# Thirty-two experts taken one at a time, in quarters of columns, instead of two at a time in halves

## The chip, the cores and the metric

The kernel runs on one core of one Trainium2 chip. The metric is the device time of one execution in microseconds; the time of a kernel is the median of its runs.

## What is computed

The reference is two layers over 512 tokens of width 1024; the change is in the first layer's mixture of experts. Each token takes its 4 best of 32 experts. An expert's gate and up weights are 1024 x 2048, its down weights 1024 x 1024, all in float32:

```
logits = xt @ w_router + b_router
top_val, top_idx = top_k(logits, 4); gates = softmax(top_val)
gate, up = split(xb @ w_gu[e] + b_gu[e])        # xb: the rows of xt that chose expert e
gate = min(gate, 7); up = clip(up, -7, 7)
hb = (up + 1) * gate * sigmoid(1.702 * gate)
yb = hb @ w_down[e] + b_down[e]                  # summed per token, weighted by its gates
```

All weights of all experts are read once from HBM: 32 x 12 MiB = 402.7 MB.

## The kernel before

An expert gets a list of at most CAP = 96 tokens, in NR = 3 rounds of ROUND = 32 rows (an expert with more would go through a second loop in `moe_exit`, behind a flag). `project_and_route` (L3433) makes the normed rows `xn`, stores them to the DRAM tensor `hidden` (512 x 1024), computes the logits with `w_router` and the table `members` of each token's rank in each expert.

`experts` (L1128) then works through 16 groups of two experts. The PE array is used as four column groups of 32 columns each: group q multiplies 32 rows (the stationary operand, 128x32) with 512 columns of weights (the moving operand) and writes 32 partitions of a PSUM bank. Before the change, the four groups are two experts times two halves of 1024 columns. For a group of experts:

- `list_rows` (L1228) multiplies one-hots of the ranks (`mark_group`, L1122, on DVE) with token numbers, and `next_index` (L1384) on DVE turns the result into row indices. POOL fetches the rows of x with one indirect DMA for each expert (L1196), 96 rows of 4 KB.
- `turn_x` (L1208) transposes x on PE against the identity, 16 transposes a group in four sets, and ACT copies the result out of PSUM (`copy_x`, L1340).
- `gate_up` (L1242): for each of 8 row blocks k, 6 banks (gate and up, three rounds) times 4 column groups, 192 matmuls; then 24 bias matmuls, four behind each bank's last block.
- `swiglu` (L1398) on DVE, with the sigmoid on ACT (L1352), in 12 DVE steps of 512 columns.
- `turn_h` (L1219) transposes h on PE, 12 transposes in three sets, and ACT copies them (`copy_h`, L1347).
- `down` (L1272): 96 matmuls of 512 columns, into the three gate banks; `copy_y` (L1414) copies them out on DVE, and ACT's queue stores them to `expert_table` (`y_out`, L1357) in four DMAs of 192 KB, pieces of 2 KB.

PE's order is written out by hand: `step` (L1295) runs `gate_up` of group e with the list of group e+1 and the transposes of h of group e-1 hooked in, then `down` of group e-1 with the transposes of x of group e+1 hooked in.

Weights come in units of 1 MiB through SP's queue (L1176) into 12 slots: six of the ring that the whole kernel shares (`weight_ring`) and six more (`more_weights`). A load waits until PE has released its slot (`ring.used`); PE releases two units at a time, since it works on two experts' units at once:

```
            def landed(n, e=None):
                for i in (n, n + 1):
                    sem, count = landing(i)
```

The units of the ring after the experts' are those of the next layer (`plan`, L3752).

## Time and profile before

| | us |
|---|---|
| median of 3 runs (lowest, highest) | 2746.55 (2745.76, 2748.36) |
| the profiled execution | 2733.44 |
| its span, first to last instruction | 2731.6 |
| PE busy in it | 2548.1 (93%) |
| DVE busy | 933.4 (34%) |
| ACT busy | 701.4 (26%) |
| POOL busy | 136.8 (5%) |

The profile is of one execution. The span runs from its first to its last instruction. Busy time of PE counts from the start of a matmul to its modelled end, and matmuls overlap, so 93% is not 93% of what the array can do; what counts is how far apart matmuls start. PEld is PE's load of the stationary operand. An f32 matmul appears as two matmul records and two loads. SPq and ACTq are the instructions with which SP and ACT start DMAs. The mean granted clock of PE over the span is 0.972 of 2.4 GHz.

### The profile page before, as it was taken

Reading aid. Unit: us, or ns where it says so; the run is one execution under the profiler, and the core shown is the slowest. Engines: PE = TensorE matmul, PEld = TensorE weight load, DVE = VectorE, ACT = ScalarE, POOL = GpSimd, SP = SyncE. Lnnn points to the kernel's source line nnn. Section 1 sums busy time; section 2 is a strip of 40 time slices with the busy share of each in tenths; the row PEclk is TensorE's granted clock in tenths of the full one; section 3 lists DMA queues with packets and bytes.
Section 4 is the critical chain, followed back from the end, with each engine's and each line's share of the span. In section 5 each row is a group of like instructions: output and inputs, shape, how many; then the busy total and the mean of one; then the engine's idle time right before and its main releaser. Section 6 shows DMA issues by size and latency. Waiting matters only on the chain. (4 is left out here: it accounts for less than half of the span.)

```text
span 2731.6 us, 49644 instructions
## 1 busy us (share of the span) xinstructions
PE 2548.1 (93%) x21426; PEld 1501.2 (55%) x21426; DVE 933.4 (34%) x1449; ACT 701.4 (26%) x1275; POOL 136.8 (5%) x110
## 2 busy tenths in 40 slices
PE   8989987999999999999999789879888799899998
PEld 6658754333333333333333258656677677788887
DVE  5575253111111111111111153547645434422233
ACT  4353331000000000000000142347555223422222
POOL 0003000000000000000000010001122000000000
PEclk9989998999999999999999989999999899999999
DMA  5343223999999999999999743421100323122220
GB/s 209 116 167 128 104 83 124 401 408 406 396 393 391 393 389 394 391 390 391 389 395 394 269 162 110 169 96 54 50 4 4 136 89 139 47 93 93 103 98 31
DMA packets 115976, 587.00 MB, mean 215 GB/s; under 512 B 12640, under 2 KB 14432, under 8 KB 71200
## 3 DMA queue, kind: packets, MB, share of 16 engines
q1 hardware_dynamic: 98944, 539.07, 51.1%
q10 hardware_dynamic: 11008, 24.98, 2.5%
q0 software_dynamic: 5888, 20.97, 2.2%
q8 instruction: 106, 1.74, 0.3%
q14 instruction: 30, 0.25, 0.0%
HBM read 564.00 MB, written 20.97 MB: 214 GB/s over the span
## 5 line engine op out<-in xcount | busy, mean ns | idle before, releaser
L1261 PE MATMUL psum<-weight_ring,expert_xT 128*32 128x512 f32 x3120 | 347.8, 597 | 1.5 <-ACT expert_xT L1344 1.5
L1261 PE MATMUL psum<-more_weights,expert_xT 128*32 128x512 f32 x3024 | 347.4, 593 | 0.0
L368 DVE TENSOR_TENSOR w_low<-weight_ring,w_high 128x2048 fp32r<-128x2048 f32 (+1 forms) x92 | 213.4, 2321 | 322.6 <-ACT w_high L363 322.2
L363 ACT CAST w_high<-weight_ring 128x2048 fp32r<-128x2048 f32 (+1 forms) x88 | 166.6, 1893 | 290.5 <-PE psum L402 144.2
L1261 PEld LDWEIGHTS psum<-weight_ring,expert_xT 128*32 128x32 f32 x3120 | 99.0, 110 | 221.2 <-issue 220.8
L1402 DVE TENSOR_SCALAR gate<-psum 128x512 f32<-128x512 f32 x48 | 33.2, 692 | 540.8 <-PE psum L1268 540.8
L1261 PEld LDWEIGHTS psum<-more_weights,expert_xT 128*32 128x32 f32 x3024 | 95.5, 110 | 196.7 <-issue 190.0
L1288 PE MATMUL psum<-more_weights,expert_hT 128*32 128x512 f32 x1584 | 178.7, 594 | 0.0
L1350 ACT COPY expert_hT<-psum 128x512 f32<-128x512 f32 x48 | 28.0, 586 | 537.1 <-PE psum L1225 511.6
L1288 PE MATMUL psum<-weight_ring,expert_hT 128*32 128x512 f32 x1488 | 165.8, 594 | 0.0
L402 PE MATMUL psum<-mix_hT_high,w_high 128*128 128x512 f32 x384 | 156.0, 406 | 6.5 <-PEq L1981 3.5
L406 PE MATMUL psum<-mix_hT_high,w_low 128*128 128x512 f32 x384 | 150.9, 393 | 0.0
L405 PE MATMUL psum<-mix_hT_low,w_high 128*128 128x512 f32 x384 | 150.8, 393 | 0.0
L402 PE MATMUL psum<-ffn_x_high,w_high 128*128 128x512 f32 x352 | 138.3, 393 | 3.8 <-PEq L3258 3.8
L405 PE MATMUL psum<-ffn_x_low,w_high 128*128 128x512 f32 x352 | 137.9, 392 | 0.0
L406 PE MATMUL psum<-ffn_x_high,w_low 128*128 128x512 f32 x352 | 137.9, 392 | 0.0
L1419 DVE COPY expert_y<-psum 128x512 f32<-128x512 f32 x48 | 33.2, 691 | 280.5 <-PE psum L1288 279.6
L1288 PEld LDWEIGHTS psum<-more_weights,expert_hT 128*32 128x32 f32 x1584 | 49.1, 110 | 101.5 <-issue 97.0
L1288 PEld LDWEIGHTS psum<-weight_ring,expert_hT 128*32 128x32 f32 x1488 | 45.5, 110 | 97.3 <-issue 94.0
L1196 POOL DMA_INDIRECT expert_x<-hidden,index x32 | 38.0, 1186 | 1100.9 <-DVE index L1388 912.4
L1344 ACT COPY expert_xT<-psum 128x384 f32<-128x384 f32 x64 | 30.4, 478 | 231.0 <-PE psum L1216 231.0
L1355 ACT ACTIVATE sigmoid<-gate 128x512 f32<-128x512 f32 x48 | 30.3, 630 | 229.3 <-DVE gate L1402 229.3
(540 smaller groups left out, 4040.9 us busy)
## 6 DMA issues: line engine op xcount, KB each, us to landing
weight_ring<-in_w_gu SPq DMA_DIRECT2D x130, 1024.0 KB, 8.3
more_weights<-in_w_gu SPq DMA_DIRECT2D x126, 1024.0 KB, 7.0
more_weights<-in_w_down SPq DMA_DIRECT2D x66, 1024.0 KB, 10.1
weight_ring<-in_w_down SPq DMA_DIRECT2D x62, 1024.0 KB, 9.2
weight_ring<-in_w_in SPq DMA_DIRECT2D x35, 1024.0 KB, 5.1
weight_ring<-in_w_ada SPq DMA_DIRECT2D x24, 1024.0 KB, 4.8
weight_ring<-in_w_ffn_in SPq DMA_DIRECT2D x22, 1024.0 KB, 4.8
expert_table<-expert_y ACTq DMA_DIRECT2D x64, 192.0 KB
```

What stands on the lines that cost most here:

```text
L363: self.m.nc.scalar.copy(high, w).then_inc(self.rounded.sem, 1)
L368: self.m.nc.vector.tensor_tensor(low, w, high.bitcast(F32), ALU.subtract).then_inc(self.ready.sem, 1)
L402: ins = m.nc.tensor.matmul(out, w[0][:, k, c], x[0][:, k, 0:n], start=(k == 0), stop=False)
L405: m.nc.tensor.matmul(out, w[0][:, k, c], x[1][:, k, 0:n], start=False, stop=False)
L406: ins = m.nc.tensor.matmul(out, w[1][:, k, c], x[0][:, k, 0:n], start=False, stop=(k == ktiles - 1))
L1196: nc.gpsimd.indirect_dma_start(x[i][:, :], None, hidden, bass.IndirectOffsetOnAxis(ap=ix[0:CAP, i:i + 1], axis=0)).then_inc(gathered[i].se ...
L1261: ins = T.matmul(ps[NR * up + j][quarter(q), :], xT[:, k, i, quarter(j)], w[i][:, up * D + c * 512:up * D + (c + 1) * 512], start=(k == 0) ...
L1288: ins = T.matmul(ps[j][quarter(z), :], hT[:, q % 2 * 2 + r, j, quarter(2 * i + q // 2)], w[i][:, r * D + c * 512:r * D + (c + 1) * 512], s ...
L1344: nc.scalar.copy(xT[:, 4 * c:4 * c + 4, i, :], ps[6 + c][:, 0:4 * CAP].rearrange("p (k s) -> p k s", k=4)).then_inc(x_copied.sem, 1)
L1355: nc.scalar.activation(s[:, j, :], g[:, j, :], ACT.Sigmoid, scale=1.702).then_inc(sig_done.sem, 1)
L1402: V.tensor_scalar(g[:, j, :], ps[j][:, :], 7.0, None, ALU.min).then_inc(gate_ready.sem, 1)
L1419: V.tensor_copy(y[:, j, :], ps[j][:, :]).then_inc(y_copied.sem, 1)
```

## The change

Experts are taken one at a time. The four column groups are now four quarters of one expert's columns. The columns of a quarter are not contiguous: quarter q holds the columns 128k + 32q to 128k + 32q + 31 of every block k (`by_quarters`), so that the 32x32 block transpose of DVE puts h into the order in which `down` needs it. For x the same order is made by storing `hidden` permuted (and the router's rows with it), viewing it as 2048 quarter rows of 1 KB, and fetching quarter q of a row into partitions 32q to 32q + 31: three indirect DMAs of 128 quarter rows for each expert. DVE then turns x and h, six transposes of 128x256 an expert, and PE's transposes and ACT's copies of them go. `gate_up` uses three banks instead of six (gate in columns 0 to 255, up in 256 to 511), `down` has three banks of its own, and swiglu and y's copy run over all three banks in one instruction of 768 columns. The list needs 12 small matmuls an expert instead of 8 a group. PE releases one unit at a time. PE's order is `gate_up` of expert e, with the list of expert e+1 two units in, then `down` of expert e-1. `moe_exit` gets a reordering copy in the loop behind its flag. The core of the diff:

```diff
 def gate_up_units(dram, e):
-    return [dram["w_gu"][e(i), k * P:(k + 1) * P, :] for k in range(GUN) for i in range(EG)]
+    return [dram["w_gu"][e, k * P:(k + 1) * P, :] for k in range(GUN)]
...
+def by_quarters(z):
+    return z.rearrange("p (k q c) -> p k q c", q=NQ, c=ROUND)
+
+def mark_ranks(nc, oc, iota, members, e):
+    for j in range(NR):
+        last = nc.vector.tensor_tensor(oc[:, :, j, :].rearrange("p t (q i) -> p t q i", q=NQ),
...
+def list_rows(nc, bank, oc, tok):
+    for j in range(NR):
+        for t in range(NT):
+            last = nc.tensor.matmul(bank[:, 2 * j:2 * j + 2], oc[:, t, j, :], tok[:, 2 * t:2 * t + 2], start=(t == 0), stop=(t == NT - 1))
...
             def gather():
-                for i in range(EG):
-                    nc.gpsimd.indirect_dma_start(x[i][:, :], None, hidden, bass.IndirectOffsetOnAxis(ap=ix[0:CAP, i:i + 1], axis=0)
+                for j in range(NR):
+                    nc.gpsimd.indirect_dma_start(x[:, j, :], None, hidden, bass.IndirectOffsetOnAxis(ap=ix[:, j:j + 1], axis=0)
...
+                        if k == 0:
+                            pe.wait_ge(x_ready.sem, e * NR + x_ready.at(j + 1))
+                            if j == 0 and loop is not None:
+                                pe.wait_ge(gate_ready.sem, loop + gate_ready.at(0))
+                                pe.wait_ge(gu_freed.sem, loop + gu_freed.at(0))
+                        for q in range(NQ):
+                            ins = T.matmul(ps[j][part(q), :], xT[:, j, k, :], w[:, :, q, :], start=(k == 0), stop=False)
+                            if j == 0 and q == 0:
+                                release(ins, n0 + k)
+                    if k == GUN - 1:
+                        for j in range(NR):
+                            for q in range(NQ):
+                                ins = T.matmul(ps[j][part(q), :], sel[:, :], by_quarters(bias[:, :])[:, :, q, :], start=False, stop=True)
...
+                            for q in range(NQ):
+                                ins = T.matmul(y_banks[part(q), j, :], hT[:, j, 2 * k + r, :], w[:, r * D + q * QD:r * D + (q + 1) * QD],
+                                               start=(k == 0 and r == 0), stop=(k == DNN - 1 and r == 1))
...
+            gate_up(0, 0, half_way=lambda: make_list(0))
+            gate_up(GUN, 1, 1, lambda: make_list(1))
+            down(GUN + GUN, 0)
+            with pe.Fori(2, LAST) as e:
+                gate_up(GUN, e, e, lambda: make_list(e))
+                down(GUN + GUN, e - 1, e)
+            gate_up(GUN, LAST, LAST)
+            down(GUN + GUN, LAST - 1, LAST)
+            down(N - DNN, LAST)
...
+            def turn_x(e):
                 for j in range(NR):
+                    dve.wait_ge(gathered[j].sem, e * 16 + gathered[j].at(16))
+                    V.transpose(xT[:, j, :, :].rearrange("p k s -> p (k s)"), x[:, j, :]).then_inc(x_ready.sem, 1)
...
+            def leave_banks(e):
+                dve.wait_ge(gu_done.sem, e + gu_done.at(1))
+                V.tensor_scalar(g[:, :, :], gate_up_banks[:, :, 0:QD], 7.0, None, ALU.min).then_inc(gate_ready.sem, 1)
+                V.tensor_scalar(u[:, :, :], gate_up_banks[:, :, QD:2 * QD], 7.0, -7.0, ALU.min, ALU.max).then_inc(gu_freed.sem, 1)
...
             with dve.Fori(1, LAST) as e:
+                next_index(e)
+                marks(bass.ds(e + 2, 1))
+                leave_banks(e)
+                turn_x(e + 1)
+                mark(bass.ds(e + 1, 1))
                 swiglu(e)
+                copy_y(e - 1)
+                turn_h(e)
...
-            sp.dma_start(wr[:, :, :].rearrange("p k e -> p (k e)"), m.dram["w_router"]).then_inc(loaded.sem, 16)
+            for k in range(KD):
+                q = slice(ROUND * (k % 4), ROUND * (k % 4) + ROUND)
+                sp.dma_start(wr[q, k // 4:KD:2, :], m.dram["w_router"].rearrange("(q c) (k e) -> k c q e", q=NQ, k=KD)[k]).then_inc(loaded.sem, 16)
...
-                    V.scalar_tensor_tensor(xn[t % 2][:, half(h)], m.X[:, t, half(h)], stat[:, t, 4:5], row[:, half(h)],
-                                           ALU.mult, ALU.mult).then_inc(scaled.sem, 1)
+                    for q in (2 * h, 2 * h + 1):
+                        last = V.scalar_tensor_tensor(xn[t % 2][:, q * QD:(q + 1) * QD].rearrange("p (k c) -> p k c", k=KD),
+                                                      by_quarters(m.X[:, t, :])[:, :, q, :], stat[:, t, 4:5], by_quarters(row[:, :])[:, :, q, :],
+                                                      ALU.mult, ALU.mult)
+                    last.then_inc(scaled.sem, 1)
```

## Rows read from the trace of the kernel before

**Rows 1.** The page, the span in 40 slices of 68.3 us each.

```profile
GB/s 209 116 167 128 104 83 124 401 408 406 396 393 391 393 389 394 391 390 391 389 395 394 269 162 110 169 96 54 50 4 4 136 89 139 47 93 93 103 98 31
```

**Rows 2.** Waits of PE and of SP's queue, 500 to 1580 us: total, times, longest.

```profile
PE psum L1225 <- ACT expert_hT L1350: 2.8, 1, 2.8
...
SPq L1176 <- PE psum L1261: 511.4, 120, 8.6
```

**Rows 3.** Windows: length, busy time (instructions) of each engine, PEclk, DMA share, GB/s.

```profile
480.00:700.00 220.00, 218.86 (x2056) 70.79 (x2052) 39.24 (x67) 19.34 (x35) 6.89 (x6) 1.00 1.02 407
700.00:1500.00 800.00, 800.00 (x7436) 254.78 (x7432) 124.72 (x212) 63.88 (x115) 25.28 (x22) 1.00 1.00 392
```

**Rows 4.** Timeline of SP's queue, 455 to 720 us: start, length, instruction.

```profile
461.15 0.33 SPq L1176 DMA_DIRECT2D weight_ring<-in_w_gu  x1
...
554.43 13.07 SPq L1176 DMA_DIRECT2D more_weights<-in_w_gu  x6
...
622.79 13.07 SPq L1176 DMA_DIRECT2D more_weights<-in_w_gu  x6
```

**Rows 5.** Timeline of PE and its loads in one group, and at the stage's end.

```profile
1281.94 0.66 PE L1225 MATMUL psum<-ident,up 128*128 128x128 f32 x4
...
1287.82 0.66 PE L1225 MATMUL psum<-ident,up 128*128 128x128 f32 x4
...
1300.66 0.40 PE L1268 MATMUL psum<-bias,sel_gu 96*32 96x512 bf16 x4
...
1301.74 0.40 PE L1268 MATMUL psum<-bias,sel_gu 96*32 96x512 bf16 x4
...
1313.66 0.55 PE L1216 MATMUL psum<-ident,expert_x 96*128 96x96 f32 x4
...
1316.85 0.55 PE L1216 MATMUL psum<-ident,expert_x 96*128 96x96 f32 x4
...
1332.57 0.13 PEld L1261 LDWEIGHTS psum<-weight_ring,expert_xT 128*32 128x32 f32 x4 [0.30 <-issue]
...
1333.99 0.16 PEld L1261 LDWEIGHTS psum<-more_weights,expert_xT 128*32 128x32 f32 x8
...
1334.44 0.13 PEld L1261 LDWEIGHTS psum<-more_weights,expert_xT 128*32 128x32 f32 x4 [0.30 <-issue]
...
1334.87 0.13 PEld L1261 LDWEIGHTS psum<-more_weights,expert_xT 128*32 128x32 f32 x4 [0.30 <-issue]
...
1539.99 15.63 PE L1288 MATMUL psum<-more_weights,expert_hT 128*32 128x512 f32 x144
```

**Rows 6.** Timeline of PE in other stages.

```profile
100.13 0.39 PE L3210 MATMUL psum<-w_high,hT_high 128*128 128x512 f32 x1
...
101.49 0.39 PE L3210 MATMUL psum<-w_high,hT_high 128*128 128x512 f32 x1
...
125.47 1.07 PE L1824 MATMUL psum<-weight_ring,silu_c 128*32 128x256 f32 x16
...
2200.49 0.39 PE L402 MATMUL psum<-mix_hT_high,w_high 128*128 128x512 f32 x1
...
2201.85 0.39 PE L402 MATMUL psum<-mix_hT_high,w_high 128*128 128x512 f32 x1
```

**Rows 7.** A window of the recurrence, in the columns of rows 3.

```profile
2000.00:2010.00 10.00, 9.27 (x314) 8.11 (x312) 5.39 (x13) 6.10 (x19) 5.64 (x6) 1.00 0.01 3
```

**Rows 8.** DMA, 460 to 700 us: packets, MB, share; issues, us to landing.

```profile
q0 software_dynamic: 896, 3.15, 4.1%
q10 hardware_dynamic: 896, 1.57, 1.8%
...
expert_x<-hidden,index POOLq DMA_INDIRECT x8, 10.6
```

**Rows 9.** Groups by form, 530 to 1560 us: busy, mean ns | idle before.

```profile
L1402 DVE TENSOR_SCALAR gate<-psum 128x512 f32<-128x512 f32 x45 | 31.1, 692 | 513.2 <-PE psum L1268 513.2
...
L1196 POOL DMA_INDIRECT expert_x<-hidden,index x26 | 29.9, 1149 | 858.8 <-DVE index L1388 854.8 <-issue 4.0
```

More of the change, by code:

```diff
@@ L62 @@
 DNN = 4
-GROUPS = E // EG
 EXTRA = 6
@@ L1235, in landed @@
-            def landed(n, e=None):
-                for i in (n, n + 1):
-                    sem, count = landing(i)
-                    pe.wait_ge(sem, count if e is None else (e - 1) * (16 * LOOP // SLOTS) + count)
-                return slot(n), slot(n + 1)
-            def gate_up(n0, group, e=None, hook=lambda k: None):
+            def landed(n, e=None):
+                sem, count = landing(n)
+                pe.wait_ge(sem, count if e is None else (e - 1) * (16 * LOOP // SLOTS) + count)
+                return slot(n)
@@ L1244, in gate_up, with release @@
+            def release(ins, n):
+                if n > 0 or U0 > 0:
+                    ins.then_inc(ring.used, 1)
+            def gate_up(n0, e, loop=None, half_way=lambda: None):
                 for k in range(GUN):
[L1245 to L1248 removed]
+                    w = by_quarters(landed(n0 + k, loop))
+                    if k == 2:
+                        half_way()
@@ L1352, in sigmoid @@
-            def sigmoid(group):
-                for j in range(NR):
-                    act.wait_ge(gate_ready.sem, group * NR + gate_ready.at(j + 1))
-                    nc.scalar.activation(s[:, j, :], g[:, j, :], ACT.Sigmoid, scale=1.702).then_inc(sig_done.sem, 1)
-            def y_out(group, e):
-                act.wait_ge(y_copied.sem, group * NR + y_copied.at(NR))
-                for z in range(4):
-                    i, c = z // 2, z % 2
-                    dst = table[e(i), :, c * 512:c * 512 + 512]
-                    dst = dst.rearrange("(j p) n -> p j n", p=ROUND) if len(dst.shape) == 2 else dst.rearrange("a (j p) n -> p (a j) n", p=ROUND)
-                    act.dma_start(dst, y[quarter(z), :, :]).then_inc(y_stored.sem, 16)
@@ L1365, in _, with sigmoid, y_out @@
-            copy_x(0)
+            def sigmoid(e):
+                act.wait_ge(gate_ready.sem, e + gate_ready.at(1))
+                nc.scalar.activation(s[:, :, :], g[:, :, :], ACT.Sigmoid, scale=1.702).then_inc(sig_done.sem, 1)
+            def y_out(n, e):
+                act.wait_ge(y_copied.sem, n + y_copied.at(1))
+                for q in range(NQ):
+                    dst = table[e, :, q * QD:(q + 1) * QD]
+                    dst = dst.rearrange("a (j p) n -> p (a j) n", p=ROUND) if len(dst.shape) == 3 else dst.rearrange("(j p) n -> p j n", p=ROUND)
+                    act.dma_start(dst, y[part(q), :, :]).then_inc(y_stored.sem, 16)
@@ L1414, in copy_y @@
-            def copy_y(group, e=None):
-                for j in range(NR):
-                    dve.wait_ge(down_done.sem, group * NR + down_done.at(j + 1))
-                    if j == 0 and e is not None:
-                        dve.wait_ge(y_stored.sem, group * 64 + y_stored.at(0))
-                    V.tensor_copy(y[:, j, :], ps[j][:, :]).then_inc(y_copied.sem, 1)
-            dve.sem_inc(y_copied.sem, NR)
-            dve.sem_inc(y_stored.sem, 1)
-            mark(slice(0, EG))
-            mark_ranks(slice(EG, 2 * EG))
@@ L3528, in _ @@
             pe.wait_ge(onehot.sem, onehot.at(1))
-            for i in range(EG):
-                for t in range(NT):
-                    last = T.matmul(ps[5][0:CAP, 2 * i:2 * i + 2], oc[:, t, i, :], tok[:, 2 * t:2 * t + 2], start=(t == 0), stop=(t == NT - 1))
-            last.then_inc(listed.sem, 1)
+            list_rows(nc, ps[5], oc, tok).then_inc(listed.sem, 1)
         @block.scalar
@@ L3593, in _ @@
             V.memset(members[:, :, E:E + 2], 0.0)
+            for q in range(NQ):
+                V.memset(quarter[ROUND * q:ROUND * q + ROUND, :], float(q))
             def copy_turned(t):
```

333 lines of the change are left out of this document (121 added, 212 removed).

## The prediction

> **What bounds the kernel now.** I read the page first for where the time lies. In the slices of GB/s [rows 1] one stage stands out: for some 1100 of 2731.6 us the core moves about 390 GB/s. That is the expert stage, 16 groups of two experts, the only stage whose loops change. There I read the waits [rows 2]. TensorE (PE) waits once, 2.8 us for a copy of h at the very end; the SP queue waits 511.4 us for PE's gate and up matmuls alone, that is, for slots to come free. So PE sets the pace and weights wait for it. The windows [rows 3] say how near the loads are to being the bound: PE is busy throughout, and the 16 DMA engines show 1.00 to 1.02. From 480 to 700 us, while the late start of the loads was caught up, they moved 407 GB/s; later, when SP had to wait, 392. I take 407 as what they can do with this mix and 392 as what PE asks for. Third, the period: SP's issues repeat 554.43 to 622.79 [rows 4], 68.36 us a group.
>
> The PE timeline [rows 5] splits that period. An f32 matmul is two records; four records, one for each column group, start each 0.43 us (1334.44 to 1334.87). A group of experts has 288 matmuls, 576 records, 144 rounds of 0.4295 = 61.8 us. The rest is what PE does in between:
> - h transposes: 1281.94 to 1287.82 is 5.88 us for 48 records (12 rounds, 5.15) and one set of transposes: 0.73, three times, 2.2 us.
> - x transposes: 1313.66 to 1316.85 is 3.19 for 24 records (6 rounds, 2.58): 0.61, four times, 2.4 us.
> - bias: 1300.66 to 1301.74 is 1.08 for 2 rounds (0.86) and 4 bias matmuls: 0.22, six times, 1.3 us.
> - the list of rows: 1332.57 to 1334.44 is 1.87 for 3 rounds (1.29): 0.58.
>
> Sum 68.3, against 68.36. It closes, so PE's stage is counted out.
>
> **The change on PE.** Per pair of experts:
> - Gate and up: 96 matmuls an expert of 512 columns, 192 a pair, as before: 384 records, 96 rounds, 41.2 us, if the moving operand costs the same. It is now 16 runs of 32 columns. The nearest rows are the wide tiles, whose moving operand is two runs of 256: six records in 1.36 us (100.13 to 101.49), exactly as the unbroken L402, six in 1.36 (2200.49 to 2201.85) [rows 6]. One break costs nothing. From the other side, 0.227 less the 0.215 of a pass here is 0.012 us, the most one break could have cost, were the unbroken row slow for another reason. I take zero, and keep 12 ns a break.
> - Down: 192 matmuls of 256 columns in place of 96 of 512, 96 rounds of half the columns. From below a round is half of 0.43, 0.215; from above it is a quarter of L1824's 1.07 us, in which 16 records of just this shape run, the last one's way out of the array included [rows 6]: 0.27. I take 0.215, since that tail comes once a group and not once a round: 20.6 us, as before; at 0.27 it would be 25.7.
> - Bias: 24 matmuls, 1.3 us. Lists: 12 matmuls where 8 cost 0.58, so 0.87, twice a pair, 1.7 us.
> - The x and h transposes, 4.6 us, leave PE.
>
> Sum 64.9: 3.5 us less, over 16 pairs 56 us. That is what PE alone would give.
>
> Down's records now go out twice as often, one load and one matmul record each 54 ns. A stretch of small matmuls shows 314 records and 312 loads in 10 us [rows 7], 32 ns, so I cost the issue at nothing. The Trainium skill ("TensorE: Matmul & The Clock Gate", on decode and dispatch) gives about 62 ns per MATMUL where the sequencer decodes in software; by that, down would be 384 x 62 ns = 23.8 us, PE 68.1, and the gain near nothing. By that rule the trace does not go here: it shows half of that.
>
> **The change on the loads.** A pair moves 24 weight units (25.17 MB), 0.79 MB of x and 0.79 MB of y: 26.7 MB, at 407 GB/s 65.7 us. So the next thing to be late is the weights, just behind PE's 64.9. Pieces shrink to 1 KB: x from 192 pieces of 4 KB to 768, y from 384 of 2 KB to 768. The queue rows [rows 8] cover 240 us times 16 engines: ACT's stores take 1.8%, 69 us, for 768 data packets of 2 KB, 90 ns each or 44 ns per KB; the fetches 4.1%, 157 us, for 768 packets of 4 KB, 205 ns or 50 ns per KB (the other 128 packets of each are completion counts; I give them no time). A 1 KB piece costs at least its bytes, 41 to 45 ns, and at most what a 2 KB one does, 90. At the upper end: 384 more stores (35 us) and 768 x 90 - 192 x 205 = 30 us of fetches, 65 over 16 engines, 4.0 us a pair. At the lower end nothing. Time has been near the bytes in both rows, so I take 0.2 us: 65.9 us a pair, with 65.7 and 69.7 as ends.
>
> From the first issue of the stage at 461.15 [rows 4], when five units are in place, 379 units (397.4 MB), 31 experts' x (12.2) and 30 experts' y (11.8) must move before the last unit is in: 421.4 MB / 407 GB/s = 1035 us, plus 3 for the pieces and 2 for the first landing, so 1501; PE uses the last unit in 2.6: 1504. PE's last matmul now ends at 1539.99 + 15.63 = 1555.6 [rows 5]. So 51.6 us by the loads, 56 less the start-up below by PE.
>
> **What moves to other engines.** VectorE (DVE) does the turning: six block transposes of 256 columns an expert. DVE's 512-column PSUM read is 0.69 us [rows 9], so some 0.35 each, and 1.0 for each of the five 768-column steps; with marks and index near 9.5 us of 32.5. Its order puts the x turning between the bank copies and the swiglu, and y's copy ahead of the h turning: h for expert e is ready about 2 us into gate_up(e+1) and wanted 20 us later. ACT loses its 7 copies a group. Costed at nothing under PE's 32 us an expert.
> The x chain is the one to watch. The list of expert e+1 runs two units into gate_up(e), 5.2 us; index by about 7; POOL's three fetches at 1.15 us [rows 9] and the gaps between, the last issued near 10; landing 10.6 us after issue [rows 8], so 21. DVE turns x near 24, PE wants it at 32. Cover: 8 us. SP issues 12 loads an expert one slot at a time, unhindered.
> Once only: gate_up(1) follows gate_up(0) with no down between, so two bank copies and one turning are bare: 2.0 + 0.35 and the handshakes, 2.7 us lost. Before the last down, y's copy and a turning (1.4 us) stand where transposes and their copies stood: nothing. Ahead of the first gate_up, longer marks and a longer list (0.3 on PE, some 1 on DVE) stand against four sets of x transposes and their copies that go (2.4): nothing. The router table comes as eight small loads: seven more issues on SP, ahead of weights needed 70 us later, and perhaps 2 us for DVE under a PE tile; the four xn steps for two: nothing.
>
> **Sum.** PE 56 - 2.7 = 53; loads 52. The two paces meet so closely that each will now and then wait for the other; I take 50 us. Against the profiled execution, 2733.44 us (its span 2731.6), that is 2683.4. It ran 13.1 us under the median of the three runs; the forecast for the median is 2746.55 - 50 = 2696.5 us. Less than 0.2%, 5.5 us, I call no change.
>
> **Rivals.**
> - **Broken reads slow the gate and up matmuls: slower.** Place: the moving operand in 1536 rounds (16 pairs x 96), each with 30 breaks (15 in each pass). At the bound of 12 ns a break: 0.36 us a round, +553 us, 2746.6 - 50 + 553 = 3250. It decides from 50/1536 = 33 ns a round, 1.1 ns a break. For: no row has runs so short. Against: the wide tiles. The Trainium skill ("Advanced Engine Details and Errata", Memory Cachelines) says that any non-contiguous access pattern significantly slows matmuls, though under PSUM; under SBUF it speaks of 16-byte lines and asks for two hits on each. Here PSUM stays contiguous and a run is 128 bytes, so its SBUF rule would leave the time alone. 0.10.
> - **Small pieces fill the queues.** At 69.7 us a pair the loads pass today's 68.36, +21 us less the start's credit: about 2760. Break-even is 68.2, some 2.5 us a pair, 40 engine-us over 960 more pieces, 42 ns each. For: 1.02 of share is already used. Against: 44 and 50 ns per KB in pieces of 2 and 4 KB. Over break-even 0.07; around it, no change, 0.06; part of the gain eaten (2715 to 2741), 0.12.
> - **The three fetches land late.** If a landing grew to 10.6 us for each fetch one after the other, x is in at 7 + 32 = 39, turned at 40, 8 us after PE wants it: 32 x 8 = 256 us, about 2950. For: three where two were, 128 pieces each. Against: 10.6 us is what they took in the stretch in which the weights' own queue ran at its full 407 GB/s [rows 3, 8]. 0.04.
> - **Issue binds down: slower.** At the upper bound of 0.27 a round, 25.7 us, PE's pair is 70.0 against 68.36: 16 x 1.6 + 2.7, about 2775. It decides from 0.25 a round, 62 ns a record. For: L1824 shows no more than four rounds in a row. Against: rows 7. (The software decode that the Trainium skill describes, cited above, would end just there.) 0.01.
> - **PE and loads as summed.** 2682 to 2715: 0.60.
>
> **Numbers.** Faster 0.60 + 0.12 = 0.72; same 0.06; slower 0.10 + 0.07 + 0.04 + 0.01 = 0.22. The range runs from all of PE's gain and a little at the start, 2680, to the packets' upper end, 2765; outside are most of the broken-read, issue and fetch cases, under 0.2.
>
> **What would show it.** In the changed profile: no L1216 or L1225 transposes; rounds of 0.43 us in gate and up and 0.215 in down; SP's period near 32.8 us an expert; GB/s near 407 through the whole stage and first PE waits for weights, short ones. Wrong would be: rounds over 0.46 us in gate and up (broken reads); GB/s under 400 with SP no longer waiting for PE (pieces); PE or DVE waiting on expert_x (fetches).

## The result and the profile after

The changed kernel takes 2669.08 us (median of four runs, 2661.5 to 2671.59) against 2746.16 before: a ratio of 0.9718, 95% interval 0.9693 to 0.9742, so 77 us less, give or take 7. The forecast was 2696.5 with a range of 2680 to 2765. The sign was right and the result lies below the range. The profiled executions, 2733.44 and 2661.5 us, differ by 71.9; the traces account for that, and the further 5.1 us between the medians are scatter of single executions.

The page's GB/s slices of the changed kernel answer to [rows 1], and its windows (in the columns of [rows 3]) to [rows 3]:

```profile
GB/s 204 111 178 139 111 42 102 414 416 417 416 417 416 417 416 416 416 416 416 416 416 416 299 114 80 190 72 43 45 4 47 111 91 127 56 102 95 95 95 32
```

```profile
480.00:700.00 220.00, 217.61 (x2720) 87.31 (x2716) 62.89 (x121) 6.67 (x8) 21.23 (x21) 1.00 1.02 416
700.00:1400.00 700.00, 700.00 (x8896) 284.95 (x8891) 193.03 (x373) 17.78 (x22) 66.71 (x66) 1.00 1.02 416
```

The stage moves 416 GB/s in both windows; 407, which the prediction took for the loads' limit, is passed at once. The waits of TensorE and, in a second fence, of SP's queue answer to [rows 2] (waited for: us in all, times, longest):

```profile
PE psum L1254 <- DVE expert_xT L1337: 9.2, 2, 6.8
PE psum L1497 <- PEq L1188: 6.4, 1, 6.4
...
PE psum L1538 <- DMA exit_b_down<-in_b_down: 2.7, 1, 2.7
```

```profile
SPq L1198 <- PE psum L1254: 524.4, 252, 7.5
SPq L1198 <- PE psum L1274: 246.0, 120, 2.2
```

TensorE waits for no weight in the whole stage. Its 9.2 us are the first turned x of the stage (6.8) and the bare hand-over at the second expert (2.4). SP still waits for TensorE. The timeline of TensorE at the stage's first matmul, through one expert in its middle, and at its end answers to [rows 5]:

```profile
456.79 7.54 PE L1254 MATMUL psum<-weight_ring,expert_xT 128*32 128x512 f32 x48 [6.79 <-DVE expert_xT L1337]
...
901.10 5.33 PE L1254 MATMUL psum<-more_weights,expert_xT 128*32 128x512 f32 x48
906.37 0.45 PE L1145 MATMUL psum<-tok,rank_onehot 128*128 128x2 bf16 x12
906.75 5.36 PE L1254 MATMUL psum<-more_weights,expert_xT 128*32 128x512 f32 x48
911.92 10.48 PE L1254 MATMUL psum<-weight_ring,expert_xT 128*32 128x512 f32 x96
922.22 0.83 PE L1260 MATMUL psum<-bias,sel_gu 96*32 96x512 bf16 x12
922.88 5.36 PE L1274 MATMUL psum<-weight_ring,expert_hT 128*32 128x256 f32 x96
928.06 5.36 PE L1274 MATMUL psum<-more_weights,expert_hT 128*32 128x256 f32 x96
933.24 5.33 PE L1254 MATMUL psum<-more_weights,expert_xT 128*32 128x512 f32 x48
...
1480.64 10.57 PE L1274 MATMUL psum<-more_weights,expert_hT 128*32 128x256 f32 x192 [1.48 <-DVE expert_hT L1361]
1497.63 1.92 PE L1497 MATMUL psum<-ident,dense_gates 128*32 128x128 f32 x16 [6.42 <-PEq L1188]
1502.28 3.79 PE L1538 MATMUL psum<-exit_b_down,exit_gates_T 32*128 32x512 f32 x8 [2.73 <-DMA exit_b_down<-in_b_down]
```

The steps can be read off. Gate and up: 96 records in 10.30 us (911.92 to 922.22), 24 rounds of 0.429, as before the change, though the operand is now in runs of 32 columns. Down: 96 records in 5.18 us (922.88 to 928.06), 24 rounds of 0.216, half of 0.43. An expert takes 901.10 to 933.24, 32.14 us: 64.3 a pair where 68.36 stood [rows 4]. From the first expert matmul to the end of the last, the stage is 456.79 to 1491.21, 1034.4 us, against 459.23 to 1555.62, 1096.4, before. I call this the length of the stage. It is read from one execution of each kernel, but it repeats far better than the whole time: where nothing in the stage should change, it comes out the same to 0.2 us (1096.4 and 1096.3, 1024.0 and 1023.8 below).

So 62.0 of the 71.9 us come from the stage. The start differs by 2.4, which is scatter (over all runs below it lies between 451.9 and 462.5). The remaining 7.5 come behind the stage, all but 0.1 of them in two waits right behind it, where the kernel before had (timeline of TensorE, the answers to the last two rows above):

```profile
1564.81 1.92 PE L1548 MATMUL psum<-ident,dense_gates 128*32 128x128 f32 x16 [9.19 <-PEq L1166]
1574.10 3.79 PE L1589 MATMUL psum<-exit_b_down,exit_gates_T 32*128 32x512 f32 x8 [7.37 <-issue]
```

The last stores are waited for 2.8 us less, and the matmuls of the exit bias 4.6 us less. What these two are worth is taken up at the end.

The transfers from 460 to 700 us answer to [rows 8]:

```profile
q0 software_dynamic: 1152, 3.15, 3.5%
q10 hardware_dynamic: 2688, 2.36, 2.9%
...
more_weights<-in_w_gu SPq DMA_DIRECT2D x34, 1024.0 KB, 17.7
...
expert_x<-hidden,index POOLq DMA_INDIRECT x24, 5.8
```

The same 3.15 MB of x took 4.1% of the engines before and take 3.5% now, in fewer packets than its 3072 pieces of 1 KB: 24 x 16 = 384 of the 1152 are counts, as before, which leaves 768 packets of 4 KB. The pieces are packed together. A fetch, now a third of the bytes, lands 5.8 us after its issue, not 10.6. Weights land 17.7 us after theirs, some seven units of 1 MB queued at 2.5 us each. The loads are close behind TensorE.

### The profile page after: what moved, and what is told of

Same layout as the page of the kernel before. It is cut to its first block and busy times, and to the rows that moved or that the text cites. A ratio compares the mean times of both kernels' runs of the same rounds, so it can differ in the third digit from the quotient of the medians.

```text
span 2659.7 us, 55822 instructions
## 1 busy us (share of the span) xinstructions
PE 2483.8 (93%) x24306; PEld 1570.6 (59%) x24306; DVE 1042.5 (39%) x1703; ACT 640.1 (24%) x1147; POOL 196.5 (7%) x174
## 5 line engine op out<-in xcount | busy, mean ns | idle before, releaser
L1301 ACT ACTIVATE sigmoid<-gate 128x768 f32<-128x768 f32 x32 | 27.0, 843 | 991.3 <-DVE gate L1343 991.3
L1343 DVE TENSOR_SCALAR gate<-psum 128x768 f32<-128x768 f32 x32 | 30.7, 958 | 451.8 <-PE psum L1260 451.8
L1274 PE MATMUL psum<-more_weights,expert_hT 128*32 128x256 f32 x3168 | 176.8, 379 | 1.5 <-DVE expert_hT L1361 1.5
L1216 POOL DMA_INDIRECT expert_x<-hidden,index x96 | 98.3, 1024 | 1060.0 <-DVE index L1326 855.6
L1274 PE MATMUL psum<-weight_ring,expert_hT 128*32 128x256 f32 x2976 | 166.3, 379 | 0.0
L1274 PEld LDWEIGHTS psum<-more_weights,expert_hT 128*32 128x32 f32 x3168 | 103.9, 110 | 68.7 <-issue 1.9
L1274 PEld LDWEIGHTS psum<-weight_ring,expert_hT 128*32 128x32 f32 x2976 | 96.3, 110 | 64.7
L1356 DVE COPY expert_y<-psum 128x768 f32<-128x768 f32 x32 | 30.6, 957 | 185.1 <-PE psum L1274 185.1
L402 PEld LDWEIGHTS psum<-mix_hT_high,w_high 128*128 128x128 f32 x384 | 73.0, 190 | 27.4 <-issue 12.7
L405 PEld LDWEIGHTS psum<-mix_hT_low,w_high 128*128 128x128 f32 x384 | 72.9, 190 | 17.4 <-issue 2.6
## 6 DMA issues: line engine op xcount, KB each, us to landing
weight_ring<-in_w_gu SPq DMA_DIRECT2D x130, 1024.0 KB, 17.4
more_weights<-in_w_gu SPq DMA_DIRECT2D x126, 1024.0 KB, 17.7
more_weights<-in_w_down SPq DMA_DIRECT2D x66, 1024.0 KB, 18.9
weight_ring<-in_w_down SPq DMA_DIRECT2D x62, 1024.0 KB, 18.2
weight_ring<-in_w_in SPq DMA_DIRECT2D x35, 1024.0 KB, 5.8
weight_ring<-in_w_ada SPq DMA_DIRECT2D x24, 1024.0 KB, 4.9
weight_ring<-in_w_ffn_in SPq DMA_DIRECT2D x22, 1024.0 KB, 4.8
```

The lines of the kernel that those rows point to most:

```text
L402: ins = m.nc.tensor.matmul(out, w[0][:, k, c], x[0][:, k, 0:n], start=(k == 0), stop=False)
L405: m.nc.tensor.matmul(out, w[0][:, k, c], x[1][:, k, 0:n], start=False, stop=False)
L1216: nc.gpsimd.indirect_dma_start(x[:, j, :], None, hidden, bass.IndirectOffsetOnAxis(ap=ix[:, j:j + 1], axis=0)).then_inc(gathered[j].sem, 16)
L1274: ins = T.matmul(y_banks[part(q), j, :], hT[:, j, 2 * k + r, :], w[:, r * D + q * QD:r * D + (q + 1) * QD], start=(k == 0 and r == 0), sto ...
L1301: nc.scalar.activation(s[:, :, :], g[:, :, :], ACT.Sigmoid, scale=1.702).then_inc(sig_done.sem, 1)
L1343: V.tensor_scalar(g[:, :, :], gate_up_banks[:, :, 0:QD], 7.0, None, ALU.min).then_inc(gate_ready.sem, 1)
```

## The experiments

The theory after this reading: TensorE sets the pace of the changed kernel, and 407 GB/s was no property of the loads but held the cost of the old fetch of x. Rivals: the loads still bind, at 416; or 407 came from something else in the old order. All runs follow, with the stage's length from each trace, from the start of the first expert matmul to the end of the last. The ratio is to the kernel before, run beside it.

| Run | Median us | Ratio, 95% interval | Stage us |
|---|---|---|---|
| before | 2746.16 | 1 | 1096.4 |
| after | 2669.08 | 0.9718 (0.9693 to 0.9742) | 1034.4 |
| a_no_bias | 2664.24 | 0.9704 (0.9674 to 0.9734) | 1024.1 |
| a_short | 2661.97 | 0.9714 (0.9680 to 0.9747) | 1024.0 |
| a_rows4k | 2682.44 | 0.9779 (0.9738 to 0.9819) | 1044.0 |
| a_short_rows4k | 2682.33 | 0.9773 (0.9744 to 0.9802) | 1043.1 |
| b_no_turns | 2688.28 | 0.9813 (0.9781 to 0.9846) | 1049.3 |
| b_no_turns_quarters | 2669.81 | 0.9737 (0.9716 to 0.9758) | 1032.2 |
| b_quarters | 2741.16 | 0.9995 (0.9977 to 1.0012) | 1096.3 |
| a_short_fixed1k | 2668.05 | 0.9719 (0.9674 to 0.9765) | 1023.8 |
| a_short_rows3k | 2670.24 | 0.9749 (0.9728 to 0.9770) | 1020.7 |
| a_short_split4k | 2701.38 | 0.9834 (0.9785 to 0.9883) | 1055.2 |
| a_short_part96 | 2683.40 | 0.9800 (0.9756 to 0.9845) | 1042.8 |
| a_short_down8k | 2658.83 | 0.9682 (0.9634 to 0.9729) | 1015.5 |
| a_down8k | 2716.17 | 0.9892 (0.9846 to 0.9937) | 1074.1 |
| a_list4 | 2668.75 | 0.9744 (0.9724 to 0.9763) | 1032.0 |
| a_pairs | 2667.95 | 0.9734 (0.9714 to 0.9754) | 1034.4 |
| a_pairs_list4 | 2668.24 | 0.9740 (0.9717 to 0.9763) | 1031.8 |

### How far are the loads behind TensorE?

**a_no_bias**: the bias matmuls of the experts are left out.

```diff
-  ... xT[:, j, k, :], w[:, :, q, :], start=(k == 0), stop=False)
+  ... xT[:, j, k, :], w[:, :, q, :], start=(k == 0), stop=(k == GUN - 1))
-  for q in range(NQ):
-      ins = T.matmul(ps[j][part(q), :], sel[:, :], by_quarters(bias[:, :])[:, :, q, :], ...)
```

> The changed kernel without the twelve bias matmuls of each expert (the expert gate and up biases are left out of the result). They take some 0.6 us of TensorE's 32.14 us an expert. Theory TensorE alone sets the pace and the loads have room above 416 GB/s: 31.5 us an expert, 32 x 0.6 = 20 us less, about 2649 us, some 424 GB/s, and TensorE waits for no weights. Rival, the loads are at their limit at 416 GB/s (both meet): within 3 us of 2669, 32.1 us an expert, and TensorE waits for weights. In between (a limit near 420): about 2659.

Of the 21 us taken from TensorE (0.66 an expert) the stage gives back 10.3. The timeline shows why. Two lists that follow each other early in the stage, and two late:

```profile
521.36 0.45 PE L1145 MATMUL psum<-tok,rank_onehot 128*128 128x2 bf16 x12
...
552.84 0.45 PE L1145 MATMUL psum<-tok,rank_onehot 128*128 128x2 bf16 x12
...
1315.43 0.45 PE L1145 MATMUL psum<-tok,rank_onehot 128*128 128x2 bf16 x12
...
1347.53 0.45 PE L1145 MATMUL psum<-tok,rank_onehot 128*128 128x2 bf16 x12
```

Early an expert takes 31.48 us, TensorE's own pace without the bias, while the weights already on the chip are used up. Late it takes 32.10 (32.07 on average over the last 15), the pace of the loads, against 32.14 in the changed kernel. The two paces all but meet, and what was gained was gained early: of the twelve slots seven are queued (17.7 us at 2.5), so some four units lie ready besides the one in use, 4 x 2.5 = 10 us (an estimate), and these are spent once. The time between the two theories comes from that stock.

**a_short**: the last of eight steps of gate and up cut to one matmul of twelve.

```diff
-  for q in range(NQ):
+  for q in range(NQ if k < GUN - 1 else j == 0):
       ins = T.matmul(ps[j][part(q), :], xT[:, j, k, :], ...)
```

> The changed kernel with the last of the eight steps of each gate and up product cut to one matmul of twelve (that part of the sum is left out), every weight still loaded. TensorE then needs about 2.2 us less an expert, 59.9 us a pair of experts, so that the loads should bind and show their limit: 26.74 MB a pair. If the limit is 416 GB/s: 64.3 us a pair, no gain, 2669 us. If it is 422: 63.4 a pair, 14 us less, 2655. If there is none below 446 GB/s: 59.9 a pair, 70 us less, 2599. My theory is a limit near 422. In the case of a limit TensorE waits for weights in every expert; otherwise in none.

The window from 700 to 1400 us (columns of [rows 3]), and TensorE's waits for weights:

```profile
700.00:1400.00 700.00, 673.77 (x8420) 299.17 (x8416) 192.94 (x370) 18.58 (x22) 66.69 (x66) 1.00 1.02 417
```

```profile
PE psum L1274 <- DMA weight_ring<-in_w_down: 24.7, 26, 1.0
PE psum L1254 <- DMA weight_ring<-in_w_gu: 5.2, 24, 0.3
```

TensorE now waits for weights in 26 and 24 places and the stage is as long as without the bias, 1024.0. That is the loads' limit with this mix: 417 GB/s, not the 422 I held likeliest. It is a quarter of a per cent above what the changed kernel moves.

### Does the shape of the fetch move the limit?

**a_rows4k**: from the third expert on, one fetch of 96 whole rows at fixed places into a spare tile.

```diff
-  for j in range(NR):
-      indirect_dma_start(x[:, j, :], None, hidden, ...(ap=ix[:, j:j + 1], axis=0))
+  indirect_dma_start(spare[:, :], None, whole, ...(ap=at[0:CAP, 0:1], axis=0))
```

> The changed kernel, with the three quarter fetches of an expert replaced from the third expert on by one fetch of 96 whole 4 KB rows at fixed places into a spare tile (the same 393 KB; x keeps its old contents, so the experts compute on old rows). Theory: the 407 GB/s of the kernel before held the cost of this fetch shape. Then the fetches dent the loads again, 26.74 MB / 407 = 65.7 us a pair, 16 x 1.4 = 23 us more, about 2692, and TensorE waits for weights after fetches. Rival, the shape of the fetch costs the loads nothing and 407 came from elsewhere: 2669 within 3 us, 416 GB/s, no wait for weights.

**a_short_rows4k**: both edits together.

> Both edits of the two runs before together: the last step of each gate and up product cut to one matmul of twelve, and one fetch of 96 rows of 4 KB in place of three of 128 quarter rows. With TensorE at about 59.9 us a pair the loads bind, so the cost of the fetch shape stands free of TensorE. Theory fetch shape: 407 GB/s, 65.7 us a pair, some 37 us above the run with the short step and quarter fetches if that one is at 422 GB/s. Rival, the shape costs nothing: within 3 us of that run.

The same window of the one and of the other:

```profile
700.00:1400.00 700.00, 694.49 (x8816) 281.44 (x8812) 193.21 (x373) 17.83 (x22) 24.18 (x22) 1.00 1.02 408
```

```profile
700.00:1400.00 700.00, 663.84 (x8294) 294.95 (x8290) 188.30 (x363) 17.73 (x21) 23.13 (x21) 1.00 1.02 409
```

Same bytes, same order, same weights: 408 and 409 GB/s in place of 416 and 417. With the short step the stage grows from 1024.0 to 1043.1, 19 us (expected 37 from a limit of 422 that was not there). a_rows4k loses 9.6 us in the stage where 23 were expected, since TensorE again lives on its stock at first. The theory holds: the old fetch costs the loads 2% more than the new one. The queues' shares from 700 to 1400 us tell where it falls: the weights' queue takes 95.3% of the 16 engines' time for 274.36 MB in a_short and 94.8% for 269.62 MB in a_short_rows4k, which is 38.9 and 39.4 us of one engine for each MB; the fetches' queue takes 40 and 47. With 12.58 MB of weights and 0.39 MB of x an expert, more than half of the cost lies in the weights' own packets.

The same from the other side. **b_no_turns** takes the transposes alone out of the kernel before.

```diff
-  for k in range(4):
-      last = T.transpose(ps[6 + c][:, k * CAP:(k + 1) * CAP], x[i][...], ...)
-  last.then_inc(x_turned.sem, 1)
+  return x_turned      # counted up by the next matmul; h likewise
```

> The kernel before with TensorE's transposes of x and h left out of its loop (the copies to xT and hT then take what lies in the banks, so the experts compute on old data); waits, copies, fetches of 4 KB rows and loads stay. TensorE alone would then need about 63.7 us a pair of experts in place of 68.4. Theory: with the fetch of before the loads go to 409 GB/s, 26.74 MB / 409 = 65.4 us a pair, some 15 x 3.0 = 45 us less than the kernel before. Rival, the loads go to 417 here too: 64.1 us a pair, 64 us less. Rival, TensorE alone: 63.7, 70 us less.

**b_no_turns_quarters** adds quarter rows:

```diff
-  indirect_dma_start(x[i][:, :], None, hidden, ...(ap=ix[0:CAP, i:i + 1], axis=0))
+  for j in range(NR):
+      indirect_dma_start(spare[:, i, j, :], None, whole, ...(ap=at[:, 0:1], axis=0))
```

> The same, and from the third pair on x is fetched as six fetches of 128 quarter rows (1 KB, fixed places, into a spare tile) in place of two of 96 rows of 4 KB. Theory, the fetch shape sets the limit of the loads: 417 GB/s, 64.1 us a pair, about 64 us less than the kernel before and some 19 us less than the run with whole rows. Rival, the shape matters only beside the rest of the change: equal to that run within 4 us.

**b_quarters** has the new fetches and keeps the transposes.

> The kernel before with its transposes, and only the fetches replaced by six of 128 quarter rows at fixed places into a spare tile from the third pair on (the experts compute on old rows). TensorE sets the pace of before at 68.4 us a pair, 391 GB/s, below either limit. Theory: equal to the kernel before within 4 us. Rival, the loads already bound before: up to 20 us less.

Lists of b_no_turns that follow each other, early and late, and those of b_no_turns_quarters:

```profile
516.60 0.52 PE L1236 MATMUL psum<-tok,rank_onehot 128*96 128x2 bf16 x8
...
580.31 0.52 PE L1236 MATMUL psum<-tok,rank_onehot 128*96 128x2 bf16 x8
...
1296.31 0.52 PE L1236 MATMUL psum<-tok,rank_onehot 128*96 128x2 bf16 x8
...
1361.59 0.52 PE L1236 MATMUL psum<-tok,rank_onehot 128*96 128x2 bf16 x8
```

```profile
515.54 0.52 PE L1251 MATMUL psum<-tok,rank_onehot 128*96 128x2 bf16 x8
...
579.25 0.52 PE L1251 MATMUL psum<-tok,rank_onehot 128*96 128x2 bf16 x8
...
1280.66 0.52 PE L1251 MATMUL psum<-tok,rank_onehot 128*96 128x2 bf16 x8
...
1344.92 0.52 PE L1251 MATMUL psum<-tok,rank_onehot 128*96 128x2 bf16 x8
```

Without transposes TensorE needs 63.71 us a pair at first, as the prediction's counts give (68.3 less 4.6). But with the old fetch the loads hold it to 65.28 later and only 47 us of the stage are gained (1049.3). With quarter rows it keeps 63.71 until near the end, when the stock is used up and a pair takes 64.26, and 64 are gained (1032.2), as much as the whole change gives (62.0), with the old stores and the old order of loads. Quarter rows alone give nothing (1096.3), since TensorE needs 68.36. Neither part does the work alone: the transposes take TensorE off the path, and the new fetch lets the loads follow.

### What in the fetch costs the loads?

All with the short step, so that the loads bind. **a_short_fixed1k** is the control: three fetches of 128 quarter rows at fixed places.

> A control for the runs with fixed rows: the short last step, and three fetches of 128 quarter rows of 1 KB per expert as in the changed kernel, but at fixed places and into a spare tile. Theory, the shape of the fetch counts and not which rows it takes: equal to the run with the short step alone within 4 us, 417 GB/s. Rival, fixed rows spread over the table are what costs: near the run with one fetch of 96 whole rows, 20 us more.

**a_short_split4k**: three fetches of 32 rows of 4 KB.

> The short last step, and the 96 whole rows of 4 KB fetched by three fetches of 32 rows each instead of one of 96 (fixed places, spare tile). If it is the 4 KB row into one partition that costs the loads: 408 GB/s, as with one fetch of 96, 20 us more than with quarter rows. If it is one large fetch that takes all its packets at once: near 417 GB/s, within 5 us of the run with quarter rows. My chance for the row is six in ten.

**a_short_rows3k**: one fetch of 128 rows of 3 KB.

> The short last step (one matmul of twelve in the last step of gate and up), and one fetch of 128 rows of 3 KB at fixed places into a spare tile, the same 393 KB on all 128 partitions. If the length of the row taken by one partition is what costs the loads: near 408 GB/s, some 15 to 20 us above the run with the short step and quarter rows. If it is that a fetch of 96 or 32 rows leaves partitions out: 417 GB/s, within 5 us of that run.

**a_short_part96**: four fetches of 96 partitions in 1 KB pieces.

```diff
+  for j in range(NQ):
+      indirect_dma_start(spare[:, j, :], None, whole, ...(ap=at[0:CAP, 0:1], axis=0))
```

> The short last step, and the same 393 KB fetched by four fetches of 96 partitions, each partition taking 1 KB quarter rows at fixed places (spare tile), in place of three fetches of 128. If leaving partitions out is what costs the loads: the stage from the first expert matmul to the last takes some 1043 us as with 96 rows of 4 KB (with 128 partitions it was 1024 with quarter rows and 1021 with rows of 3 KB), 20 us more in all, near 2682. If it is the 4 KB row: 1024 us, near 2665.

The window from 700 to 1400 us of each, in this order:

```profile
700.00:1400.00 700.00, 674.91 (x8392) 297.80 (x8388) 194.12 (x374) 18.58 (x22) 66.74 (x66) 1.00 1.02 417
```

```profile
700.00:1400.00 700.00, 654.81 (x8178) 290.60 (x8174) 186.03 (x357) 17.75 (x21) 58.94 (x63) 1.00 1.02 403
```

```profile
700.00:1400.00 700.00, 674.26 (x8432) 303.09 (x8428) 194.86 (x374) 18.58 (x22) 25.15 (x22) 1.00 1.02 418
```

```profile
700.00:1400.00 700.00, 663.33 (x8270) 293.58 (x8266) 190.16 (x366) 17.72 (x21) 83.36 (x87) 1.00 1.02 409
```

The control is as long as a_short (417 GB/s, 1023.8 against 1024.0): fixed places and the spare tile cost nothing. The length of the row, for which I gave six chances in ten, is not it: 3 KB rows on 128 partitions cost no more than 1 KB rows there (418 GB/s, the stage 1020.7), and 1 KB pieces on 96 partitions cost as much as 4 KB rows on 96 (409, 1042.8). Which rows are read is not it either: part96 takes the first 96 of the 128 quarter rows that the control takes. With 32 rows in a fetch it is worse (403, 1055.2, where I expected 408 or 417). Its three fetches go to three different sets of 32 partitions, so that an expert's bytes lie on the same 96 partitions as with one fetch of 96: what counts is how many partitions one fetch takes. Against fetches of all 128, the same 393 KB an expert cost 19 us more over the stage in fetches of 96 partitions and 31 in fetches of 32. That it is the partitions of a fetch is shown for 128 and 96, since on either the length of the row and the number of fetches could be changed at next to no cost; for 32 it rests on one run. How they cost the loads is not shown.

The Trainium skill ("SBUF — State Buffer", on the DMA port swizzle) says that a transfer's rate depends on how many of sixteen ports its partitions reach, and that the first 64 partitions lie on eight of them. By that, a fetch of 32 rows loads eight ports alone, and one of 96 loads these twice as much as the others. The order of the four runs agrees; no run shows the ports.

### Longer pieces for down

**a_short_down8k** and **a_down8k** give each partition two neighbouring rows of w_down, 8 KB, and let TensorE read every second column of gate and up to match.

```diff
-  ... z.rearrange("a (c p) n -> p (a c) n", p=P)
+  ... z.rearrange("a (p c) n -> p (a c n)", p=P)
-  return z.rearrange("p (k q c) -> p k q c", q=NQ, c=ROUND)
+  return z.rearrange("p (k q c r) -> p q k r c", q=NQ, c=ROUND, r=2)
```

> The changed kernel with its short last step (one matmul of twelve, as before), and the w_down units laid so that a partition takes two neighbouring rows, 8 KB in one piece, in place of two of 4 KB; gate and up columns are read in pairs to match (every second column, 8 bytes apart). Theory: the loads bind this kernel and pieces of 8 KB go faster, as the gate and up units do: about 422 GB/s, 63.4 us a pair, 12 us below the run with the short step alone. Rival, the limit does not depend on the piece: equal within 4 us. Rival, TensorE reads columns 8 bytes apart at half its rate: then it binds and the run is hundreds of us longer.

> The changed kernel with all its matmuls, and only the w_down units in pieces of 8 KB with gate and up columns read in pairs; nothing is left out. Theory: TensorE takes 64.2 us a pair by itself, so that a higher limit of the loads gives back next to nothing: within 4 us of the changed kernel, with transfers that land sooner after their issue than its 17 to 19 us. Rival, the loads alone set the pace of the changed kernel: 12 us less. Rival, reads 8 bytes apart slow TensorE: hundreds of us more.

The window of a_short_down8k, then one group of matmuls from 700 to 1400 us in a_down8k and in the changed kernel (busy, mean ns | idle):

```profile
700.00:1400.00 700.00, 699.55 (x8561) 313.09 (x8550) 196.85 (x378) 18.57 (x22) 66.70 (x66) 1.00 1.02 420
```

```profile
L1259 PE MATMUL psum<-more_weights,expert_xT 128*32 128x512 f32 x2016 | 236.7, 615 | 0.0
```

```profile
L1254 PE MATMUL psum<-more_weights,expert_xT 128*32 128x512 f32 x2112 | 235.2, 593 | 0.0
```

The first expectation holds in its direction: 420 GB/s (422 expected), and the stage 8.5 us shorter (12 expected); the medians alone would not tell. But TensorE, slowed by the new columns, sets the pace at 31.47 us an expert for most of this stage, and the loads only at its end, at some 31.8; that 420 is their limit is confirmed by a_pairs below, which moves the same. The second fell. Columns 8 bytes apart lengthen a record from 593 to 615 ns and the stage by 40 us, 1.24 an expert: not half the rate, but enough for TensorE to lose more than the loads gain.

### Is there a faster version?

**a_list4** makes the list with four matmuls of 96 columns, **a_pairs** keeps the 8 KB pieces but reads runs of 64 columns and lets VectorE pick every second column of h as it turns it, **a_pairs_list4** does both.

```diff
-  list_rows(nc, ps[6], oc, tok)
+  for t in range(NT):
+      matmul(ps[6][:, 0:CAP], tw[:, t, :], one[:, t, :], start=(t == 0), stop=(t == NT - 1))
```

```diff
-  V.transpose(hT[:, j, :, :]..., u[:, j, :])
+  V.transpose(hT[:, j, :, :]..., u[:, j, :].rearrange("p (k c r) -> p k r c", c=ROUND, r=2))
```

> The changed kernel with an expert's list made by four bf16 matmuls of 96 columns (token numbers as the held side, spread so that each quarter of the bank gets them) and one turn by VectorE, in place of twelve of two columns; nothing is left out. The list's 0.57 us of TensorE an expert should fall to about 0.3. Theory that both bounds lie at the same place (TensorE 64.3 us a pair, loads 26.74 MB / 417 GB/s = 64.1): at most 0.2 x 16 = 3 us less, about 2666, within the spread. Rival, TensorE alone sets the pace: 0.27 x 32 = 9 us less, 2660.

> The changed kernel with w_down in 8 KB pieces, and the order put right by VectorE, which turns every second column of h, while TensorE reads runs of 64 columns of gate and up; nothing is left out. The loads' limit rises from 417 to 420 or 421 GB/s (63.6 us a pair). Theory of two bounds at the same place: TensorE stays at 64.3, so no gain, within 3 us of 2669. Rival, the loads alone set the pace: 0.6 x 16 = 10 us less, 2659.

> Both edits together: TensorE some 63.7 us a pair, loads 63.6. Theory of two bounds at the same place: only now does the time fall, by 0.6 x 16 = 9 us, to about 2660, and the whole is more than the two single runs add up to. Rival, one bound alone: equal to the one of the two single runs that gained.

The list of a_list4 and the matmul behind it, and the window and the landing time of a weight unit in a_pairs from 700 to 1400 us:

```profile
906.35 0.34 PE L1286 MATMUL psum<-one_rank,tok_wide 128*128 128x96 bf16 x4
906.62 5.36 PE L1256 MATMUL psum<-more_weights,expert_xT 128*32 128x512 f32 x48
```

```profile
700.00:1400.00 700.00, 700.00 (x8920) 284.96 (x8912) 194.91 (x374) 18.52 (x22) 66.70 (x66) 1.00 1.02 420
...
more_weights<-in_w_gu SPq DMA_DIRECT2D x88, 1024.0 KB, 11.7
```

a_pairs relieves the loads (landing 11.7 us in place of 17.7) and its stage is 1034.4, to the tenth that of the changed kernel: its time is TensorE's, and the loads, at 420 GB/s, only get further ahead. The list shrank from 0.38 to 0.27 us up to the next matmul, not to 0.3 from 0.57, so a_list4 gains 2.4 us in the stage (at most 3 expected) and the two together 2.6, where I expected 9: TensorE is still the bound. That last expectation was wrong by the size of the list's saving. The medians of the three lie within 1.2 us of the changed kernel's, far inside their scatter: no version was found that is measurably faster.

## Why the prediction was wrong

**What the miss is made of.** The forecast was 50 us, the medians differ by 77.1: 62.0 in the stage, 7.5 behind it, and some 7.6 of scatter (2.4 at the start, 5.1 between the profiled executions and the medians). The stage alone would have put the median at 2684.5, inside the range. In the sum, TensorE's 53 and the loads' 52 were both too small, and the smaller of the two sets the time: with either one alone put right, the forecast would hardly have moved.

**The limit of the loads: wrong, and the main miss.** The step that failed is "I take 407 as what they can do with this mix". The 407 was read with the kernel before's own fetch in the mix [rows 3, 8], and the change removes that fetch. The limit is 417 (a_short) with the new fetch and 408 to 409 with the old shape (a_rows4k, a_short_rows4k, and b_no_turns in its late pairs: 26.7 MB / 65.28 us). The window of the 407 also begins in the start of the loads; behind it the kernel before moved 409 (in the columns of [rows 3]):

```profile
530.00:600.00 70.00, 70.00 (x656) 22.62 (x656) 11.15 (x19) 6.15 (x11) 2.29 (x2) 1.00 1.02 409
600.00:700.00 100.00, 100.00 (x940) 31.96 (x936) 19.01 (x32) 9.00 (x16) 2.30 (x2) 1.00 1.02 409
```

So two of the ten GB/s are the window, and eight the fetch. The loads need 64.1 us a pair and not 65.9. In the prediction's sum, 421.4 MB at 417 in place of 407 are 25 us less, and the loads end near 1479 and not at 1504; in a_short, where they bind, the last matmul ends at 1479.5 (that close by luck, since the starts of the runs alone differ by several us). The bounds went wrong with it: for the new pieces I set "at the lower end nothing", and so excluded a gain without a reason. The new fetch was a gain, 19 us over the stage where the loads bind, because each fetch takes all 128 partitions.

**TensorE's sum: the mechanism right, one term mis-sized.** Rounds of 0.43 and half of that, the bias, the transposes and the gap at the start (2.4 for 2.7) came out as counted. The list was costed at 0.87 us, as 8 matmuls' 0.58 scaled to 12. It costs 0.50: from 901.10 to 906.75 are 5.65 us, of which 12 rounds of 0.429 are 5.15. Twelve of the new matmuls take less time (0.45) than eight of the old (0.52). They hold 128 columns and not 96, and the load of these takes 96 ns and not 125, which scaling by the count left out; that this is the reason is not tested. With 41.2, down's 20.7, 1.3 and two lists of 0.50 the sum is 64.2; a pair measures 64.27 and not 64.9. Over 16 pairs that is 65 us less than before and not 56; less 2.4 at the start it makes 63, and 62.0 is what the stage gained.

**"The two paces meet": right, at another place.** They meet at 64.3 us a pair and not at 64.9 and 65.9: 64.27 for TensorE, 64.1 for the loads (a_short, 32.06 an expert late in the stage). TensorE is the later one and has some four units in stock, so it never waits, and the 2 or 3 us that I took off for the meeting were not lost.

**Costed at nothing, and not nothing: the exit.** The prediction says that TensorE waits once; the two waits behind the stage, 9.2 and 7.4 us, are longer than that one and were left out. Of the 7.4 us that they shrank by, 2.8 fit stores of one expert in place of two, though this wait is 9.3 to 10.4 in the runs of the changed kernel in which the loads bind (a_no_bias, a_rows4k, a_short and its variants, all with stores of one expert). Nothing ties the other 4.6 to the change. The exit bias is waited for 7.0 to 8.0 us in the kernel before, in b_quarters and in six runs of the changed kernel (a_short and its variants other than a_short_fixed1k), and 2.2 to 3.4 in the changed kernel itself and the nine other runs, b_no_turns with the exit of before among them. So it goes neither with the transposes nor with the exit's code. A long one and a short one, of a_short and a_short_fixed1k, which leave out the same matmuls:

```profile
1498.47 3.78 PE L1538 MATMUL psum<-exit_b_down,exit_gates_T 32*128 32x512 f32 x8 [7.04 <-issue]
```

```profile
1498.25 3.78 PE L1550 MATMUL psum<-exit_b_down,exit_gates_T 32*128 32x512 f32 x8 [2.73 <-DMA exit_b_down<-in_b_down]
```

In each of the eight long waits one packet of a DMA queue of kind instruction, q8, is moved (in the kernel before it is the only one of q8 from 1566.73 to 1574.10 us); in none of the ten short ones is there any. That TensorE waits there for its own instructions fits, but is not shown. In this comparison the 4.6 us look like luck.

**The rivals.** Broken reads: did not come at runs of 128 bytes (0.429 us a round). Small pieces: for x the opposite came. y's stores do go in packets of 1 KB (2688 less 384 counts are 2304 for 2.36 MB), and these take 48 ns each (2.9% of 240 us times 16), near the lower bound of 41 to 45 and far from the upper of 90. Late fetches: 5.8 us to land, not 10.6. Issue in down: rounds of 0.216. Neither did the 62 ns per MATMUL appear that the prediction quotes from the Trainium skill ("TensorE: Matmul & The Clock Gate"): a record starts every 54 ns.

## What to carry to other kernels

A transfer rate read from a trace is the limit of that mix of transfers; ask what of the mix the change removes before using it as a ceiling for the kernel after. When two bounds lie within a per cent, cost each alone, and test each with a run that relieves only the other: a kernel with a few matmuls fewer shows the loads' limit, and one with lighter loads shows TensorE's. Read the pace late in the stage: here a stock of four units hid the loads' limit for half of it and more. Each fetch of a side transfer beside saturated loads should take all 128 partitions, whatever the length of its rows.

## What the runs showed of the hardware

- The same 393 KB fetched beside saturated loads cost 0.6 us an expert more in fetches of 96 partitions than in fetches of 128, and 1.0 more in three fetches of 32 partitions each (19 and 31 us over 32 experts). Rows of 1 KB and 3 KB on 128 partitions differ by 3 us over the stage.
- Weight units with 8 KB in one piece for each partition raise the limit of the whole mix from 417 to 420 GB/s (a_short_down8k, a_pairs); a third of the weights' bytes changed.
- TensorE reads an f32 moving operand in runs of 128 bytes at full rate (24 rounds in 10.30 us), and of single columns 8 bytes apart 1.24 us an expert slower, 26 ns for each of its 48 rounds. The Trainium skill ("Advanced Engine Details and Errata", Memory Cachelines) asks for two hits on each 16-byte line of SBUF; a stride of 8 bytes still has two, so by that rule it would be free. The measurement differs and decides.
- VectorE turns a 128x256 f32 tile in 413 ns, be it of neighbouring columns (the changed kernel) or of every second column (a_pairs).
